# Up products of the first block: tokens in the array, 512 weights moved, gated rows turned by DMA

## What is computed

```python
def swiglu(y, w_in, w_out):
    a, b = jnp.split(y @ w_in, 2, axis=-1)
    return (jax.nn.silu(a) * b) @ w_out

mod = (sc @ w_mod[l] + b_mod[l]).reshape(-1, N_MOD, D_MODEL)
x = ada_out(x, swiglu(ada_in(x, mod, 0, norm_pre[l, 0]), ffn_w_in[l, 0], ffn_w_out[l, 0]), ...)
xc = ada_out(xc, swiglu(ada_in(xc, modc, 0, norm_pre[l, 0]), ffn_w_in[l, 0], ffn_w_out[l, 0]), ...)
```

## Time and profile before

| what | value |
| --- | --- |
| three runs | 1986.09 us median, 1985.05 to 1986.77 |
| the profiled execution | 1985.42 us |
| its span | 1983.6 us |
| busy in the span | PE 1949.8 us, PEld 1654.2, DVE 1368.4, ACT 1148.8, POOL 78.7 |
| granted TensorE clock | full in every slice |
| DMA | mean 206 GB/s |
| context's up groups c2 to c10 | from 56.4 to 179.7 us |
| latent up groups with what lies between them | from 242.3 to 402.9 us |

### The profile page before, as it was taken

The page is one execution under the profiler, slowest core; times in us unless marked ns, Lnnn a source line. Parts: engine busy times, 40 slices in busy tenths (PEclk is TensorE's granted clock), DMA queues, the critical chain, the costliest instruction groups (busy, mean ns, idle before and its releaser), DMA issues.

```text
span 1983.6 us, 27313 instructions
## 1 busy us (share of the span) xinstructions
PE 1949.8 (98%) x10594; PEld 1654.2 (83%) x10594; DVE 1368.4 (69%) x2239; ACT 1148.8 (58%) x1801; POOL 78.7 (4%) x147
## 2 busy tenths in 40 slices
PE   7999999999999999999999999999999999999998
PEld 5988899987878888888997788888888898778887
DVE  4457676666777666665698896665666587987663
ACT  4345465545665556665646756655665646666662
POOL 0000000001110000000100000000000100000000
PEclk9999999999999999999999999999999999999999
DMA  9797756666368967766543467775877534358771
GB/s 338 253 309 246 258 177 185 202 244 211 128 214 235 275 208 221 213 204 233 192 141 127 148 213 218 222 224 163 244 204 244 192 122 160 125 197 245 203 218 64
DMA packets 340256, 407.64 MB, mean 206 GB/s; under 512 B 67740, under 2 KB 234076, under 8 KB 340128
## 3 DMA queue, kind: packets, MB, share of 16 engines
q1 hardware_dynamic: 277616, 379.62, 57.6%
q10 hardware_dynamic: 59056, 16.91, 5.6%
q0 software_dynamic: 3456, 9.37, 1.5%
HBM read 390.40 MB, written 1.05 MB: 197 GB/s over the span
## 4 chain that ended last, share of the span: by engine, by line
PE 80%; DVE 9%; ACT 5%; DMA 3%; issue 2%; POOL 0%; SPq 0%; DVEq 0%; POOLq 0%; ACTq 0%
PE bank L989 20%; PE bank L991 20%; PE bank L990 20%; PE bank L953 19%; DMA raw<-in_ffn_w_in 2%; DVE junk L2958 2%; DVE wlo L2226 2%; DVE wlo L2237 1%; ACT whi L1567 1%; PE bank L1038 1%; ACT whi L1577 1%; DMA raw<-in_w_mod 1%; ACT gate L2159 1%; DVE tm L3117 0%; ACT junk L1632 0%
## 5 line engine op out<-in xcount | busy, mean ns | idle before, releaser
L2226 DVE TENSOR_TENSOR wlo<-raw,whi 128x1024 fp32r<-128x1024 f32 x358 | 428.4, 1223 | 234.1 <-ACT whi L1567 229.7
L1567 ACT ACTIVATE whi<-raw 128x1024 fp32r<-128x1024 f32 x360 | 369.0, 1052 | 293.1 <-PE bank L991 115.4
L989 PE MATMUL bank<-whi,xTh 128*128 128x512 f32 (+1 forms) x1344 | 525.4, 391 | 2.5 <-DVE xTl L2300 2.3
L991 PE MATMUL bank<-whi,xTl 128*128 128x512 f32 (+1 forms) x1344 | 520.2, 387 | 0.0
L990 PE MATMUL bank<-wlo,xTh 128*128 128x512 f32 (+1 forms) x1344 | 519.8, 387 | 0.0
L2237 DVE SCALAR_TENSOR_TENSOR wlo<-raw,cols,whi 128x512 fp32r<-128x512 f32 (+1 forms) x592 | 401.2, 738 | 147.7 <-ACT whi L1577 147.5
L1577 ACT ACTIVATE whi<-raw,cols 128x512 fp32r<-128x512 f32 (+1 forms) x592 | 374.4, 702 | 100.6 <-PE bank L991 35.4
L989 PEld LDWEIGHTS bank<-whi,xTh 128*128 128x128 f32 x1344 | 252.5, 188 | 56.5 <-DVE xTl L2300 3.2
L991 PEld LDWEIGHTS bank<-whi,xTl 128*128 128x128 f32 x1344 | 252.4, 188 | 52.0
L990 PEld LDWEIGHTS bank<-wlo,xTh 128*128 128x128 f32 x1344 | 252.6, 188 | 50.1 <-issue 0.5
L953 PE MATMUL bank<-xTh,whi 128*128 128x256 f32 x696 | 197.0, 284 | 0.0
(11 more groups left out here) (382 smaller groups left out, 2477.1 us busy)
## 6 DMA issues: line engine op xcount, KB each, us to landing
raw<-in_w_in SPq DMA_DIRECT2D x68, 1024.0 KB, 5.1
raw<-in_ffn_w_in SPq DMA_DIRECT2D x132, 512.0 KB, 5.7
raw<-in_ffn_w_gate SPq DMA_DIRECT2D x88, 512.0 KB, 3.8
raw<-in_ffn_w_up SPq DMA_DIRECT2D x88, 512.0 KB, 5.1
raw<-in_ffn_w_down SPq DMA_DIRECT2D x40, 1024.0 KB, 5.1
raw<-in_w_mod SPq DMA_DIRECT2D x36, 1024.0 KB, 5.9
raw<-in_ffn_w_out SPq DMA_DIRECT2D x30, 1024.0 KB, 6.4
raw<-in_w_out SPq DMA_DIRECT2D x12, 1024.0 KB, 5.2
```

The costliest lines, as they stand in the source:

```text
L989: e.matmul(o, hi[:, kc, sl], wh[:, c], start=at == 0 and k == 0, stop=False)
L991: ins = e.matmul(o, lo[:, kc, sl], wh[:, c], start=False, stop=fin)
L1567: e.activation(wh, raw, ACT.Copy).then_inc(m.whi_done, 1)
L2226: e.tensor_tensor(wl, raw, wh.bitcast(F32), ALU.subtract).then_inc(m.wlo_done, 1)
```

## The change

c2 to c10 and x0 to x10, 20 groups, are computed with `product`: tokens held in the array and 512 weights moved. Their gated rows stand in a new tile `hg` with tokens on partitions, are packed, turned by the transposing DMA and merged to words as in the later parts; the new tiles lie where `hwl`, `hx` and `silx` lie. `flip_of` numbers all turned groups, now 75 in place of 55. c0 and c1 and their `hide` stay. In c3 to c10 the turn stands behind the second piece of a group, in x1 to x10 behind the fourth, and the last two turns of each feed-forward stand in the down product, behind its second and seventh pieces. In c3 and in x1 it is `part` and `flip` alone. The number of weight pieces, their order and the ring are the same. The diff, with unchanged lines left out:

```diff
@@ -86,6 +86,10 @@
...
+def flip_of(f, g):
+    return g - 2 if f == "c" else NG - 2 + g if f == "x" else 2 * NG - 2 + (f - 1) * NG + g
+
+
@@ -259,7 +263,7 @@
...
-            self.widen(extra[:1], "flipped", 16 * f * NG, self.first["dn", f, 0, 0] + FLIPS[1] + 2, True)
+            self.widen(extra[:1], "flipped", 16 * flip_of(f + 1, 0), self.first["dn", f, 0, 0] + FLIPS[1] + 2, True)
@@ -602,6 +606,9 @@
...
+        words = self.at(self.h + HALF_H, "hword", [128, 22, 256])[0]
+        planes, turned = (self.nc.alloc_sbuf_tensor_at(n, [128, 8, 128], U16, offset=o + 2048 * k) for k, n in enumerate(("planes", "turned")))
+        self.first = self.hwh, self.hwl, words, self.at(f, "hg", [128, 8, 128])[0], planes, turned
@@ -685,6 +692,9 @@
...
+
+    def hidden(self, f):
+        return self.first if f in ("c", "x") else self.ffn[min(f, 2)]
@@ -1146,7 +1156,7 @@
...
-            self.product_w(("up", f, g), xT, 256, 4, 2, 512)
+            self.product([("up", f, g)], xT, 2, 4, 2, 512, self.idle)
@@ -1701,17 +1711,20 @@
...
-        planes, turned = m.ffn[min(f, 2)][4:6]
-        e.wait_ge(m.planes_done, (f - 1) * NG + g + 1)
-        if (f, g) != (1, 0):
-            e.wait_ge(m.words_done, (f - 1) * NG + g)
+        planes, turned = m.hidden(f)[4:6]
+        n = flip_of(f, g)
+        e.wait_ge(m.planes_done, n + 1)
+        if n:
+            e.wait_ge(m.words_done, n)
...
-        htok, planes = m.ffn[min(f, 2)][3:5]
-        n = (f - 1) * NG + g
+        htok, planes = m.hidden(f)[3:5]
+        n = flip_of(f, g)
+        if n == 0:
+            e.wait_ge(m.hid_done, 2)
@@ -1723,8 +1736,8 @@
...
-        hTh, _, words = m.ffn[min(f, 2)][:3]
-        n, w = (f - 1) * NG + g + 1, words[:, 2 * g:2 * g + 2, :]
+        hTh, _, words = m.hidden(f)[:3]
+        n, w = flip_of(f, g) + 1, words[:, 2 * g:2 * g + 2, :]
@@ -1828,8 +1841,23 @@
...
-        if g:
-            self.hidden(f, g - 1)
+
+    def hide_rows(self, f, g):
+
+        m, e = self.m, self.e
+        hg = m.first[3]
+        for i in range(2):
+            bank, _ = self.filled("up", f, g, i)
+            if f == "c" and g < 4:
+                self.evacuated("up", f, g - 2, 1)
+            c = 4 * (g % 2) + i
+            e.activation(hg[:, c:c + 3:2, :], bank[:, 0:256].rearrange("p (c n) -> p c n", c=2), ACT.Silu).then_inc(m.sil_done, 1)
+
+    def turn(self, f, g):
+        if flip_of(f, g) >= (0 if f == "c" else NG - 2):
+            self.words(f, g)
+        if g + 1 < NG:
+            self.part(f, g + 1)
@@ -1860,17 +1888,20 @@
...
+        self.hidden("c", 0)
...
-            self.stream(4)
-            self.hide("c", g)
+            self.stream(4, between={1: lambda: self.turn("c", g - 2)} if g > 2 else {})
+            self.hide_rows("c", g)
...
+                self.hidden("c", 1)
...
-        self.hidden("c", NG - 1)
...
+            if u in FLIPS:
+                self.turn("c", NG - 2 + FLIPS.index(u))
@@ -1889,12 +1920,11 @@
...
-            self.stream(4, between=beside.get(g, {}))
-            self.hide("x", g)
+            self.stream(4, between={**beside.get(g, {}), 3: lambda: self.turn("x", g - 2)} if g else beside[g])
+            self.hide_rows("x", g)
...
-        self.hidden("x", NG - 1)
...
-                  lambda: self.shape(("sh1", 0), 1, 0, m.xTh), 6, "x")
+                  lambda: self.shape(("sh1", 0), 1, 0, m.xTh), 6, "x", between={u: lambda n=n: self.turn("x", NG - 2 + n) for n, u in enumerate(FLIPS)})
@@ -2451,13 +2481,13 @@
...
-        hTh, hTl, words, _, _, turned, _ = m.ffn[min(f, 2)]
-        c = slice(2 * g, 2 * g + 2)
-        e.wait_ge(m.flip, 16 * ((f - 1) * NG + g + 1))
+        hTh, hTl, words, _, _, turned = m.hidden(f)[:6]
+        c, n = slice(2 * g, 2 * g + 2), flip_of(f, g) + 1
+        e.wait_ge(m.flip, 16 * n)
...
-        e.wait_ge(m.words_done, (f - 1) * NG + g + 1)
-        self.lo(hTl[:, c, :], words[:, c, :], hTh[:, c, :]).then_inc(m.ht_done, 1)
+        e.wait_ge(m.words_done, n)
+        self.lo(hTl[:, c, :], words[:, c, :], hTh[:, c, :]).then_inc(m.hid_done if f in ("c", "x") else m.ht_done, 1)
@@ -2574,8 +2604,17 @@
...
-        if g:
-            self.hidden(g - 1)
+
+    def hide_rows(self, f, g):
+
+        m, e = self.m, self.e
+        for i in range(2):
+            self.n.sil += 1
+            e.wait_ge(m.sil_done, self.n.sil)
+            bank, free = self.held("up", f, g, i)
+            c = 4 * (g % 2) + i
+            h = m.first[3][:, c:c + 3:2, :]
+            e.tensor_tensor(h, h, bank[:, 256:512].rearrange("p (c n) -> p c n", c=2), ALU.mult).then_inc(free, 1)
@@ -2606,17 +2645,19 @@
...
+        self.hidden(0)
...
-            self.stream(4)
+            self.stream(4, between={1: lambda: self.words("c", g - 2)} if g > 3 else {})
...
-            self.hide("c", g)
+            self.hide_rows("c", g)
+            if g == 2:
+                self.hidden(1)
...
-        self.hidden(NG - 1)
@@ -2630,6 +2671,8 @@
...
+            if u in FLIPS:
+                self.words("c", NG - 2 + FLIPS.index(u))
@@ -2651,15 +2694,14 @@
...
-            self.stream(4, between=beside.get(g, {}))
+            self.stream(4, between={**beside.get(g, {}), 3: lambda: self.words("x", g - 2)} if g > 1 else beside[g])
...
-            self.hide("x", g)
+            self.hide_rows("x", g)
...
-        self.hidden(NG - 1)
...
-                  lambda: self.shape(("sh1", 0), 1, 0, (m.xTh, m.xTl)), 6, "x", between={15: lambda: self.summed(12)})
+                  lambda: self.shape(("sh1", 0), 1, 0, (m.xTh, m.xTl)), 6, "x", between={15: lambda: self.summed(12), **{u: lambda n=n: self.words("x", NG - 2 + n) for n, u in enumerate(FLIPS)}})
```

## The result

| what | before | after |
| --- | --- | --- |
| median | 1985.77 us (4 runs, 1985.05 to 1986.77) | 2011.32 us (4 runs, 2009.47 to 2013.75) |
| ratio | | 1.0130, 95% interval 1.0118 to 1.0143 |
| profiled execution, its span | 1985.42, 1983.6 us | 2013.75, 2011.9 us |
| mean granted clock | 1.00 | 0.992 |

The change costs 25.6 us. Slower was forecast, but 14 us slower and not over 2009. In the spans the difference is 28.3 us. These are the page's first line, its row of PE and queue q10 (before: the earlier trace rows); then the head of the chain that ended last.

The account below looks back on a forecast made before the run. PE was taken to set the pace. Net of the matmul gain, stalls added 4.7 us in the context's part and 10 in the latent part: 1985.4 + 4.7 + 10 = 2000.1, forecast 2000 us, range 1986 to 2009.

Parts of the forecast that it names:

- Pitch: PE's 512-column matmuls in the 20 changed groups start 0.227 us apart, gaining 0.63 us a group, 12.6 us.
- The turn: On ACT and DVE, a piece behind a turn is ready 6.0 us after the piece ahead of it.
- The waits: PE stalls behind turns: 10.4 to 10.8 us in c2 to c10, 17.8 us in the latent part.
- the items of the context's part: Single stalls of PE listed for c5, c7, the norm, c8 and c9, given as 10.4 to 10.8 us in sum.
- the norm's 1.8: After c7's stalls, ACT's norm between its splits costs 1.8 us more, with less lead to cover it.
- the latent down product: A stall of 3.7 us behind the first of the last two turns.
- the keys: PE's matmul of the keys at the end of x6 waits 4.3 us for the convolution's last silu.
- The transpose's transfer: 20 transposes of 0.26 MB, 0.8 to 2.0 us each, taken as 1.4 us of delay for weights queued behind.
- Transfers bind as well: Rival: transposes make c4 to c9 transfer-bound, c part ending 4 to 5 us later; 2012 us, chance 0.06.
- The rivals on the fast side: Two rivals with smaller stalls: 1974 us (chance 0.13) and 1986 us (chance 0.07).
- The ring's lead: Rival: the lead of ACT and DVE over PE covers the turn; 1974 us, 1972 to 1981, chance 0.13.
- half waits: Rival: DVE's copy may be done before ACT arrives, nine stalls shrink 1.3 to 1.8 us each; 1986 us, chance 0.07.

Follow-up runs that it names:

- e2: The changed kernel with six of a piece's twelve matmuls done a second time ahead of five long waits (product's value changes); 2010.05 us, ratio 1.0124.
- e9: e5 with the latent input's norm behind the first piece of c7 and c8, and x5's DVE copy at the first piece; 1986.68 us.
- e8: The changed kernel with plain DMAs for the 20 new transposing ones and the packing cut into eight operations, holding ACT longer; 2003.95 us, ratio 1.0095.
- e14: e9 with plain DMAs in place of the 20 transposing ones; 1977.08 us, ratio 0.9960.
- e6: e5 with the turns of x2, x3, x4 and x10 behind the second piece, those of x5 and x6 behind the first; 2002.71 us.
- e5: The changed kernel with DVE's copy of the turned planes one piece earlier, ACT's program unchanged; 1990.64 us, ratio 1.0030.
- e1: The changed kernel with the turns of c3 to c10 behind the first piece instead of the second; 2000.25 us, ratio 1.0072.
- e12: Only latent groups changed against the kernel before, DVE's copy one piece earlier, first packing and transpose moved to x2's first piece; 1988.44 us.

## Why the prediction was right in sign and wrong in size

- **Pitch: right.** 0.227 us, 12.6 us gained by the sum. The pitch is in the traces at full clock; no run has the gain by itself.
- **The turn: right.** 5.98 us from split to split in c5, 6.0 forecast.
- **The waits: right in their sum, not everywhere in their place.** Forecast 28.4 us (10.6 + 17.8); the items of the context's part make 11.4 and not 10.6 (3.7 + 3.9 + 1.8 + 1.0 + 1.0), 0.8 us that change nothing here. From start to start less the pitch, the trace has 26.6. c5 and c7 had 3.4 each (forecast 3.7 and 3.9 with the norm's 1.8 besides), x2 1.4 (1.7), x3 3.4 (2.9), x6's fourth piece 2.2 (2.5), the latent down product 3.1 (3.7). c9 had 3.2 where I had 1.0: its weights landed at 159.65, 15.3 us after c8's modulation product had begun, and the forecast took 11.9 + 1.4 = 13.3. x10 had 0.5 where I had 2.7, and the keys 2.1 where I had 4.3. c8 had 0.7 (1.0). That the sum is so close is in part luck, since misses on both sides cancel. I had missed the context's down product altogether, 3.1 us: half of it comes behind its first turn, whose copy stands behind multiply-adds on DVE as in the latent one, half from DVE's scaling of a finished bank (`z`), which comes late.
- **The step that failed: a wait was priced by its length.** The sum had gain and waits; the third term, the matmuls at 1.2 GHz behind six of the waits, is 12.4 us. With it, 1985.4 - 12.6 + 26.6 + 12.4 = 2011.8, and with the longer first steps behind the waits, 1.8 us, 2013.6, where the profiled execution has 2013.75. The windows at 0.50 show the term; the profile before could not, with its clock full everywhere, but the waits that I forecast were of the kind that let it fall. This is a sum of what was lost, not what taking the slow clock away would bring: e2 got 2.9 us back in x0 to x10, and next to nothing in the context's part, where c7 took the time again.
- **The transpose's transfer: mis-sized.** I took 1.4 us as a delay in two groups. It sits in a stretch at a share of 0.89, and in e9 that stretch stands at 1.00. "Transfers bind as well", a rival with a chance of 0.06, gave 2012 us. That this is the measured time is luck: half of its mechanism is in e8 (at most 7.4 us) and e14 (7.8 in the context's part, with the issue and the late landings in it), but it has no slow clock. The rule that a transposing DMA is as fast as a plain one (the Trainium skill, "Advanced Engine Details and Errata", X-Bar Transpose (TRN2)) did not hold here: 0.5 to 1.2 us more of the engines' time each, 0.8 us more on the issuing queue.
- **The rivals on the fast side fell.** The ring's lead did not cover a turn, and half waits did not come: ACT did wait for DVE's copy, 1.9 us and more. But that wait was the cheapest thing to mend, and I treated it as given.

What is left open: how the 7.8 us of e14 divide between the engines' time, the shorter issue and the late landings; why e6 made x3 worse; why c7's weights landed later in e2; and what decides whether the clock falls behind a wait.

## What to carry to other kernels

When a step is spread over two engines, put the operation that the other engine waits for one piece ahead of the wait: one copy moved on DVE was worth 20.7 us of a loss of 25.6. Price a wait of TensorE by its length and, as a term that may or may not come, by what the matmuls behind it lose at the lower clock (1.3 to 2.6 us a wait here), but ask what would be awaited next before counting that as a gain. In the stretch whose transfers were at 0.89 the new DMAs were not hidden, and the transposing ones took more of the engines than plain ones of the same bytes. When a move brings nothing, it may be the second of two limits: the norm's place and the transposes each hid the other.

## What the runs showed of the hardware

- After 2.97 us without a matmul (c5) the granted clock was 0.50 for 5.7 us; after 2.02 us in x6 it fell too, and after 1.87 in c7 of e5. After 1.56 us (e2, c5) and after 1.47 and 1.35 in the context's down product it stayed at 1.00.
- The length of a wait alone does not decide it. In e1 the clock stayed at 1.00 after 3.19 us in x3 and after 2.69 in the latent down product, where in the kernel after it fell behind waits of 3.26 and 2.69 at the same places.
- A transposing DMA holds ACT's queue 1.25 us, up to 2.08 in the kernel after, a plain one of the same size 0.47.
- One transpose of e12 landed 10.3 us after its issue, one of e9 11.2 and one of e1 11.4, at a DMA share of 1.0 to 1.1; those of the kernel after take 3.0 to 8.6, median 4.5.
